# Feed-forwards: most column blocks as three 256-column matmuls per weight block, two blocks in one PSUM bank

## The reference, cut to what matters

```
D_MODEL = 1024
SEQ = 256
D_FF = 256 * ((8 * D_MODEL // 3 + 255) // 256)      # 2816

def rms_norm(x, g):
    xf = x.astype(jnp.float32)
    y = xf * lax.rsqrt(jnp.mean(xf * xf, axis=-1, keepdims=True) + EPS)
    return (y * g.astype(jnp.float32)).astype(x.dtype)

def swiglu(x, w_gate, w_up, w_down):
    return (jax.nn.silu(x @ w_gate) * (x @ w_up)) @ w_down

h = h + 0.5 * swiglu(rms_norm(h, ffn1_norm_g[layer]), ffn1_w_gate[layer],
                     ffn1_w_up[layer], ffn1_w_down[layer])
...
h = h + 0.5 * swiglu(rms_norm(h, ffn2_norm_g[layer]), ffn2_w_gate[layer],
                     ffn2_w_up[layer], ffn2_w_down[layer])
```

## Time and profile before

| | us |
|---|---|
| median of 3 runs | 1191.02 (1190.84 to 1191.08) |
| the profiled execution, whole | 1190.84 |
| its span, first to last instruction | 1189.2 |
| TensorE matmuls busy | 1179.6 (99%) |
| TensorE weight loads busy | 1044.4 (88%) |
| DVE busy | 862.4 (73%) |
| ACT busy | 677.6 (57%) |
| POOL busy | 65.6 (6%) |

### The profile page before, as it was taken

How to read it: one execution, slowest core, us unless ns; L and a number is a source line. 1 busy time by engine, 2 the same in 40 slices (tenths; PEclk the granted TensorE clock), 3 DMA queues, 4 the chain that set the end, 5 groups by cost and what they waited for, 6 DMA issues and landing times.

```text
span 1189.2 us, 18987 instructions
## 1 busy us (share of the span) xinstructions
PE 1179.6 (99%) x7592; PEld 1044.4 (88%) x7592; DVE 862.4 (73%) x1213; ACT 677.6 (57%) x1036; POOL 65.6 (6%) x86
## 2 busy tenths in 40 slices
PE   9999999999999999999999999999999999999998
PEld 8888889969888888888888888998888899779996
DVE  7877766887887767787766677677776668566875
ACT  6766654547655555655545457565554445556463
POOL 1501000200010000000000021000000000000000
PEclk9999999999999999999999999999999999999999
DMA  8865656663665556656655553256565665536450
GB/s 308 304 196 177 197 170 204 214 179 127 210 183 193 185 168 195 211 179 205 186 177 177 195 160 124 89 190 194 184 188 184 192 203 185 170 124 192 139 167 35
DMA packets 65398, 215.85 MB, mean 182 GB/s; under 512 B 8352, under 2 KB 12064, under 8 KB 65184
## 3 DMA queue, kind: packets, MB, share of 16 engines
q1 hardware_dynamic: 62608, 210.64, 55.3%
q10 hardware_dynamic: 2704, 4.02, 0.9%
HBM read 212.70 MB, written 1.93 MB: 180 GB/s over the span
## 4 chain that ended last, share of the span: by engine, by line
PE 95%; ACT 2%; DVE 1%; issue 1%; DMA 1%; SPq 0%; POOL 0%; ACTq 0%; POOLq 0%
PE psum L509 94%; DMA raw<-in_slots 1%; ACT whi L1249 1%; PE psum L918 0%; DVE wlo L1860 0%; ACT L1699 0%; ACT zob L1699 0%; DVE oa L2512 0%; PE psum L1058 0%; PE psum L878 0%; ACT qn L1568 0%; PE psum L1199 0%; PE psum L1007 0%; PE psum L968 0%; ACT pb L1568 0%
## 5 line engine op out<-in xcount | busy, mean ns | idle before, releaser
L509 PE MATMUL psum<-x,whi 128*128 128x512 f32 (+1 forms) x2512 | 633.7, 343 | 0.8 <-DVE aq L2447 0.3
L1860 DVE TENSOR_TENSOR wlo<-raw,whi 128x1024 fp32r<-128x1024 f32 (+2 forms) x402 | 474.1, 1191 | 167.6 <-ACT whi L1249 165.0
L1249 ACT CAST whi<-raw 128x1024 fp32r<-128x1024 f32 (+2 forms) x402 | 405.0, 1021 | 155.8 <-PE psum L509 150.8
L509 PE MATMUL psum<-x,wlo 128*128 128x256 f32 x1960 | 430.6, 279 | 0.0
L509 PEld LDWEIGHTS psum<-x,wlo 128*128 128x128 f32 x1960 | 366.6, 188 | 58.0 <-DVE wlo L1976 0.4
L509 PEld LDWEIGHTS psum<-x,whi 128*128 128x128 f32 x2512 | 382.2, 188 | 3.2 <-issue 1.3
L509 PE MATMUL psum<-g,whi 128*128 128x512 f32 x704 | 218.6, 392 | 0.0
L509 PEld LDWEIGHTS psum<-g,wlo 128*128 128x128 f32 x704 | 132.2, 188 | 29.5
L509 PE MATMUL psum<-whi,x 128*128 128x512 f32 (+1 forms) x512 | 140.6, 375 | 1.4 <-issue 1.4
L509 PE MATMUL psum<-g,wlo 128*128 128x256 f32 x704 | 139.0, 279 | 0.0
L509 PEld LDWEIGHTS psum<-g,whi 128*128 128x128 f32 x704 | 106.8, 188 | 0.0
(11 more groups left out here) (317 smaller groups left out, 775.8 us busy)
## 6 DMA issues: line engine op xcount, KB each, us to landing
raw<-in_slots SPq DMA_DIRECT2D x371, 512.0 KB, 4.1
raw<-in_slots SPq DMA_DIRECT2D x16, 384.0 KB, 3.4
raw<-in_slots SPq DMA_DIRECT2D x16, 256.0 KB, 2.9
h<-conv_mem SPq DMA_DIRECT2D x8, 284.0 KB, 5.5
mkv<-in_mem ACTq DMA_DIRECT2D x1, 1024.0 KB, 11.9
memt<-in_mem_cols ACTq DMA_DIRECT2D x1, 1024.0 KB, 15.1
conv_mem<-hc SPq DMA_DIRECT2D x3, 288.0 KB, 2.2
h<-conv_mem SPq DMA_DIRECT2D x4, 142.0 KB, 2.9
```

The costliest lines, as they stand in the source:

```text
L509: return pe.matmul(o, l, r, start=start, stop=stop, skip_group_check=True)
L1249: act.copy(held(B.whi[:, i % SPLIT, :], *n), held(B.raw[:, i % RAW, :], *n)).then_inc(*s.hi.now(i))
L1860: dve.tensor_tensor(held(B.wlo[:, i % SPLIT, :], *n), held(B.raw[:, i % RAW, :], *n), held(B.whi[:, i % SPLIT, :], *n).bitcast(F32), ALU.s ...
```

## The change

Two tables say which pairs of gate and up columns go in the narrow form: p = 2 to 6 in f = 0, p = 2, 3, 4 and 6 to 10 in f = 1, p = 2 to 10 in f = 2 and in f = 3. That is 5 + 8 + 9 + 9 = 31 pairs, 31 x 32 = 992 blocks. All 16 down pairs go narrow, 16 x 44 = 704 blocks. Together 1,696 of the feed-forwards' 2,112 blocks. p = 0 and p = 1 stay wide everywhere, p = 5 in f = 1, and p = 7 to 10 in f = 0.

A narrow gate pair lies whole in bank p % 2, an up pair in bank 2 + p % 2, so that two narrow pairs after each other use different banks. DVE reads them straight from PSUM: `gate_scale` and `up_mul` take the bank as an operand and wait for the slot's matmuls (`slot_used`), and down's first step does the same. For these 31 x 2 + 16 = 78 sums the ACT copy and the DVE sum are gone. TensorE waits (`read`) on the DVE step that read the bank two pairs before (or one, where forms change). The weights, their slots, splits and DMAs are as they were.

```
--- before.py
+++ after.py
@@ -39,6 +39,9 @@
 PAIRS = FF // 256
 
 LATE = 7
+
+NARROW_UP = (tuple(range(2, 7)), (2, 3, 4, 6, 7, 8, 9, 10), tuple(range(2, 11)), tuple(range(2, 11)))
+NARROW_DOWN = tuple(range(4))
 
 GAB_STEPS = (2, 2, 2, 1, 1, 2, 2, 1, 1, 1)
 
@@ -352,8 +355,8 @@
     sums = []
     for f in range(4):
         for p in range(PAIRS):
-            sums += [("gate", f, p), ("up", f, p)]
-        sums += [("down", f, p) for p in P4]
+            if p not in NARROW_UP[f]:
+                sums += [("gate", f, p), ("up", f, p)]
 
 
     s.w = [sig(f"w_in{i}", range(i, SLOTS, RAW), 16) for i in range(RAW)]
@@ -694,29 +697,47 @@
             mm(bank[7][:, i % 4 * 128:(i % 4 + 1) * 128], ones[:], ones[:], True, True)
 
 
-    def ffn(f, x, gen):
+    def read(done, part, f, p, narrow):
+
+        if p - 1 not in NARROW_UP[f]:
+            pe.wait_ge(*s.sum.at((part, f, p - 1)))
+        elif not narrow:
+            pe.wait_ge(*done.at((f, p - 1)))
+        elif p - 2 in NARROW_UP[f]:
+            pe.wait_ge(*done.at((f, p - 2)))
+
+    def ffn(f, xi, gen):
         base, F = FFN[f], B.ffn[f]
+        x = B.x[xi]
         for p in range(PAIRS):
             if f == 0 and p == LATE:
                 rows((rh[1], rl[1]), "mem0", 8, MKV0, 512, [[4], [5]])
+            narrow = p in NARROW_UP[f]
+            gate, up = (p % 2, 2 + p % 2) if narrow else (0, 2)
             if p:
-                pe.wait_ge(*s.sum.at(("gate", f, p - 1)))
+                read(s.gate, "gate", f, p, narrow)
             elif f == 1:
                 pe.wait_ge(*s.h.at((2, 0)))
             elif f == 2:
                 pe.wait_ge(*s.h.at((3, 2)))
             elif f == 3:
                 pe.wait_ge(*s.h.at((5, 0)))
-            if p:
-                cols(x, 8, up_slot(f, p), 0)
-                pe.wait_ge(*s.sum.at(("up", f, p - 1)))
-                cols(x, 8, up_slot(f, p) + 2, 2)
+            if narrow:
+                pair(xi, 0, up_slot(f, p), gate, range(4), True, False)
+                pair(xi, 0, up_slot(f, p) + 1, gate, range(4, 8), False, True)
+                read(s.mul, "up", f, p, narrow)
+                pair(xi, 0, up_slot(f, p) + 2, up, range(4), True, False)
+                pair(xi, 0, up_slot(f, p) + 3, up, range(4, 8), False, True)
+            elif p:
+                cols(x, 8, up_slot(f, p), gate)
+                read(s.mul, "up", f, p, narrow)
+                cols(x, 8, up_slot(f, p) + 2, up)
             else:
                 part(x, base, 0, range(4), True, False, gen)
                 if f in (1, 3):
                     pe.wait_ge(*s.h.at((2, 2) if f == 1 else (5, 1)))
                 elif f == 2:
-                    pe.wait_ge(*s.sum.at(("up", 1, PAIRS - 1)))
+                    pe.wait_ge(*s.mul.at((1, PAIRS - 1)))
                 part(x, base + 1, 2, range(4), True, False)
                 part(x, base + 2, 0, range(4, 8), False, True, gen)
                 part(x, base + 3, 2, range(4, 8), False, True)
@@ -726,7 +747,7 @@
             if f == 1 and p == 1:
                 pe.wait_ge(*s.kT0.at((1, 1)))
             if p == 2:
-                pe.wait_ge(*s.sum.at(("gate", f, PAIRS - 1)))
+                read(s.gate, "gate", f, PAIRS, False)
             if p == 3:
                 pe.wait_ge(*s.h.at(((1, 3, 4, 6)[f], 0)))
             down(f, F, down_slot(f, p), (4, 6, 0, 4)[p], p == 0)
@@ -743,7 +764,13 @@
                 if first and kc % 2 == 0:
                     pe.wait_ge(*s.g_hi.at((f, kc // 2)))
                     pe.wait_ge(*s.g_lo.at((f, kc // 2)))
-                t = two_blocks(b, h[:, k, :], l[:, k, :], F.g[:, kc], kc == 0, kc == 21, s.lo.at(i) if k == 0 else None)
+                for j in range(2):
+                    o, q = bank[b][:, j * S:(j + 1) * S], slice(j * 128, (j + 1) * 128)
+                    mm(o, h[:, k, q], F.gh[:, kc, :], kc + j == 0, False)
+                    mm(o, h[:, k, q], F.gl[:, kc, :], False, False)
+                    if k + j == 0:
+                        pe.wait_ge(*s.lo.at(i))
+                    t = mm(o, l[:, k, q], F.gh[:, kc, :], False, kc == 21)
             t.then_inc(*s.used.now(i))
             i += 1
 
@@ -1100,7 +1127,7 @@
 
     def second():
         X0 = (xh[0], xl[0])
-        pe.wait_ge(*s.sum.at(("up", 3, PAIRS - 1)))
+        pe.wait_ge(*s.mul.at((3, PAIRS - 1)))
         pair(0, 0, QK2, 2, range(4), True, False, "w2")
         pair(0, 0, QK2 + 1, 3, range(4), True, False)
         pair(0, 0, QK2 + 2, 2, range(4, 8), False, True, "w2")
@@ -1222,12 +1249,12 @@
                 t.then_inc(*s.tail.now((tt, j)))
 
     start()
-    ffn(0, B.x[0], "f0")
+    ffn(0, 0, "f0")
     mix_a()
-    ffn(1, B.x[1], "f1")
-    ffn(2, B.x[0], "f2")
+    ffn(1, 1, "f1")
+    ffn(2, 0, "f2")
     mix_b()
-    ffn(3, B.x[0], "f3")
+    ffn(3, 0, "f3")
     second()
 
 
@@ -1410,11 +1437,11 @@
                         gate_fn(0)
                         gate_fn(1)
                     up_rounded(0)
-                if i == 0 and p:
+                if i == 0 and p and p - 1 not in NARROW_UP[f]:
                     up_half(p - 1)
                 if i == 1 and p > 1:
                     up_rounded(p - 1)
-                if i == (2 if p else 1 if f == 0 else 3):
+                if i == (2 if p else 1 if f == 0 else 3) and p not in NARROW_UP[f]:
                     if p >= 2:
                         act.wait_ge(*s.mul.at((f, p - 2)))
                     half(("gate", f, p), up_slot(f, p) + (1 if p else 2), in_pairs(F.gr[:, p % 2, :]), 0)
@@ -1427,14 +1454,11 @@
                 use(up_slot(f, p) + i)
         for p in range(4):
             for i in range(6):
-                if p == 0 and i == 0:
+                if p == 0 and i == 0 and PAIRS - 1 not in NARROW_UP[f]:
                     up_half(PAIRS - 1)
                 if p == 0 and i == 1:
                     up_rounded(PAIRS - 1)
                 use(down_slot(f, p) + i)
-            if p >= 2:
-                act.wait_ge(*s.h.at((v, p - 2)))
-            half(("down", f, p), down_slot(f, p) + 5, in_pairs(B.htmp[:, p % 2, :]), (4, 6, 0, 4)[p])
             prep(v, p, targets)
 
 
@@ -1993,21 +2017,32 @@
         row = wide(row_of(n), 1, 2)
 
         def gate_sum(p):
+            if p in NARROW_UP[f]:
+                return
             halves(("gate", f, p), in_pairs(F.gr[:, p % 2, :]), 0)
 
         def gate_scale(p):
-            r = in_pairs(F.gr[:, p % 2, :])
+            r = q = in_pairs(F.gr[:, p % 2, :])
             if p == 0:
                 dve.wait_ge(*s.row.at(n))
-            dve.tensor_tensor(r, r, row, ALU.mult).then_inc(*s.gate.now((f, p)))
+            if p in NARROW_UP[f]:
+                dve.wait_ge(*s.used.at(up_slot(f, p) + 1))
+                q = in_pairs(bank[p % 2])
+            dve.tensor_tensor(r, q, row, ALU.mult).then_inc(*s.gate.now((f, p)))
 
         def up_sum(p):
+            if p in NARROW_UP[f]:
+                return
             halves(("up", f, p), in_pairs(F.pr[:, p % 2, :]), 2)
 
         def up_mul(p):
             r, q = F.gr[:, p % 2, :], F.pr[:, p % 2, :]
+            u = q
+            if p in NARROW_UP[f]:
+                dve.wait_ge(*s.used.at(up_slot(f, p) + 3))
+                u = bank[2 + p % 2]
             dve.wait_ge(*s.silu.at((f, p)))
-            dve.tensor_tensor(q, r, q, ALU.mult).then_inc(*s.mul.now((f, p)))
+            dve.tensor_tensor(q, r, u, ALU.mult).then_inc(*s.mul.now((f, p)))
 
         def up_rest(p):
             dve.wait_ge(*s.g_hi.at((f, p)))
@@ -2053,8 +2088,8 @@
                 use(down_slot(f, p) + i)
             tmp = in_pairs(B.htmp[:, p % 2, :])
             pair = flat(hT[:, 2 * p:2 * p + 2, :])
-            halves(("down", f, p), tmp, (4, 6, 0, 4)[p])
-            dve.scalar_tensor_tensor(out=tmp, in0=tmp, scalar=0.5, in1=row, op0=ALU.mult, op1=ALU.mult).then_inc(
+            dve.wait_ge(*s.used.at(down_slot(f, p) + 5))
+            dve.scalar_tensor_tensor(out=tmp, in0=in_pairs(bank[(4, 6, 0, 4)[p]]), scalar=0.5, in1=row, op0=ALU.mult, op1=ALU.mult).then_inc(
                 *s.dve_step.tick())
             dve.wait_ge(*s.dve_step.last())
             dve.tensor_tensor(pair, B.htmp[:, p % 2, :], pair, ALU.add).then_inc(*s.h.now((v, p)))
```

## The result

The kernel after took 1201.38 us (median; 1200.18 to 1205.49) beside 1191.05 us before (1190.84 to 1192.09), a ratio of 1.009 [1.0078, 1.0103]: 0.9% slower. The forecast was 1200.3 us. The profiled execution took 1200.59 us with a span of 1199.3.

The account below looks back on a forecast made before the run. TensorE, busy 99%, was taken to bound the kernel through distances between matmul starts. Block terms of -1.7, +7.1, +3.0 and +0.9 us gave +9.3 us on 1191.0: 1200.3 us, 8-in-10 range 1181.5 to 1203.0.

Parts of the forecast that it names:

- the sum's own terms: Narrow blocks: f = 0 -1.7 us; f = 1 to 3 gate and up +7.1, down +3.0 and +0.9; in all +9.3.
- the rival in which every narrow block is slow: All narrow blocks, f = 0 too, take the slow rhythm: +13.8 us, 1204.8 us; chance 0.07.
- Theory E: At entries, the wide form's two-kc cycle point sets the narrow rhythm; an odd number of extra kc turns it, even leaves it.
- Theory R: The rhythm belongs to the region (engines, DMAs or buffers there); extra kc or reordering turns no stretch.
- The copies and sums taken away are worth nothing: ACT loses 78 copies (45.8 us), DVE 78 sums (53.8 us); TensorE's work hides them, so the gain is nothing.
- New waits cost nothing: DVE's gate and up steps wait for TensorE's second slots, TensorE for banks two pairs back; cover suffices, cost zero.
- The price of a block: On x: wide 345.0 ns, narrow 340.0 or 353.5; narrow on g taken as on x.
- The rule of the entry: Where wide goes into narrow: last left pair spanning 0.39 us gives 340.0 ns blocks, 0.40 gives 353.5.
- that the trace of before tells how f = 0 will be entered: Last pairs of p = 1 and p = 10 in f = 0 span 0.39 us, so 336 blocks gain 1.7 us.
- quick everywhere: Rival: all narrow blocks quick, 1,520 gaining 5.0 ns and f = 2's 176 gaining 8.3: -9.1 us, 1181.9 us; chance 0.23.
- mixed: Rival: f = 1 from p = 6 and all f = 2 quick, rest as forecast: -1.6 us, 1189.4 us; chance 0.14.
- The estimate of 1195.2 us: N/2.4 + 2.5 ns per matmul: wide block 325 ns, narrow 327.5, change costs 4.2 us; the prediction set it aside.

Follow-up runs that it names:

- the other order: Kernel after with the last one or two wide kc ahead of four entries in f = 1 to 3 reordered, no work added: 1205.96 us.
- the first experiment: Kernel after with one or two extra wide kc ahead of five entries and one 256-column matmul ahead of f = 3 p = 2: 1198.98 us.

## Why f = 0 does not always come out the same

**Only f = 0 narrow.** The tables cut to f = 0, the rest in the wide form (the wide code put back for `down` of the other three).

```
-NARROW_UP = (tuple(range(2, 7)), (2, 3, 4, 6, 7, 8, 9, 10), tuple(range(2, 11)), tuple(range(2, 11)))
-NARROW_DOWN = tuple(range(4))
+NARROW_UP = (tuple(range(2, 7)), (), (), ())
+NARROW_DOWN = (0,)
```

> One part of the change alone: the narrow form in f=0 only (p=2 to 6 and down), all of f=1 to 3 wide as before. Forecast by the sum's own terms: 336 blocks x -5.0 ns = -1.7 us against before, 1189.4 us, and f=1 to 3 as long as before. If each added matmul had a cost wherever it stands (the rival in which every narrow block is slow) 336 x +8.5 ns = +2.9 us, 1194 us.

Ten executions, median 1193.95 us beside 1191.43; ratio 1.001 [0.9997, 1.0022]. They are no spread around one value but three clusters: 1188.8 (two), 1191.4 (two) and 1194.1 (six). The 1189.4 that the sum's own terms gave was met by the lowest cluster alone. The profiled execution was in the middle one, and had p = 2 to 6 slow and the down quick. 160 blocks of 13.3 ns are 2.1 us, the longer stall that starts them 0.1 (below), and 176 with the 24 that `mix_a` has behind them 2.7; by these sizes the clusters are none, one and both of f = 0's stretches slow. The two outer ones have no profile. The rival that every added matmul costs something had said 1194, which is near the median; but the quick down of the profiled execution contradicts it.

**The kernel after once more,** to see whether its own spread is this:

> The changed kernel, unchanged, for the spread of its times. If its f=0 falls either way in each execution (first stretch 160 blocks, second 176 and 24 of mix_a, 13.3 ns each), the times lie in clusters near 1200.3 (both quick), 1202.6 (one slow) and 1205.2 us (both slow). If something else scatters it, they lie in between as well.

1201.28 us (1200.72 to 1205.91), before beside it 1191.28; ratio 1.0092 [1.0073, 1.0111]. The profiled execution was the one of 1205.91. Its timeline around the break ahead of slot 7, where TensorE turns the norm row, and at the entry behind it:

```profile
26.54 0.39 PE L512 MATMUL psum<-x,wlo 128*128 128x256 f32 x2
26.92 0.43 PE L674 MATMUL psum<-ident,small 128*128 128x128 f32 x2
...
29.75 0.40 PE L512 MATMUL psum<-x,wlo 128*128 128x256 f32 x2
29.98 0.40 PE L512 MATMUL psum<-x,whi 128*128 128x256 f32 x2
...
85.81 0.40 PE L512 MATMUL psum<-x,whi 128*128 128x256 f32 x2
```

and the same break in the first profile of after:

```profile
27.41 0.40 PE L512 MATMUL psum<-x,wlo 128*128 128x256 f32 x2
27.65 0.38 PE L674 MATMUL psum<-ident,small 128*128 128x128 f32 x2
```

From the left pair to the row's matmul it is 0.38 us here and 0.24 there. These 0.14 us of waiting for the norm row turn the restart, the last left pair of p = 1 spans 0.40 in place of 0.39, and 160 blocks run at 55.83 us / 158 = 353.4 ns. The other profiles of kernels with x at these addresses agree: where the distance is 0.23 or 0.24 us (before, after, and the kernel with f = 0 wide below) p = 1 ends at 0.39; where it is 0.37 to 0.39 (this one, f = 0 alone, the other order, two nudges) it ends at 0.40, and in the first experiment, with 0.36 and one `kc` more, at 0.39. The down of f = 0 was slow too (at the break ahead of slot 45 the restart differed by some 3 ns), f = 1 to 3 were as in the first profile. So a stall that no table of waits lists costs 2 us, through the rhythm behind it. Both stretches slow are 5 us, and two of after's eight executions are 5 us above the lowest (1205.5, and the profiled 1205.9); five lie at 1200.2 to 1201.6. The one of 1202.16 has no profile, and I can't say which stretch it is. Why the highest cluster holds six of ten executions with f = 0 alone narrow, and two of eight here, is open.

## What the rhythm is worth once it is set by hand

**Two nudges.** The kernel after with one wide `kc` more ahead of p = 2 of f = 1 and of f = 3. f = 2 gets none; by the first run it should be handed the quick rhythm by f = 1.

```
+NUDGE = {105: 'dup1', 273: 'dup1'}
...
```

The code that reads the table is that of the first experiment.

> The changed kernel with one extra wide kc (4 matmuls into a free bank, never read, 0.7 us) ahead of f=1 p=2 and one ahead of f=3 p=2, nothing else. Theory E with what the first job showed (the quick rhythm is handed on from the narrow down of f=1 through the wide p=0 and p=1 of f=2): f=1, f=2 and f=3 all run at 0.340 us a block. Against before: 1,184 blocks x -5.0 ns and 176 x -8.3 ns in f=1 to 3 = -7.4 us, +1.4 us for the extra work, and f=0 as it falls: -1.7 us with both of its stretches quick, +0.6 with one slow, +2.9 with both slow. So times in three clusters at 1183.6, 1186 and 1188.3 us, median 1186 to 1188. Theory R: 1202 us or more.

1187.45 us (1185.51 to 1188.15) in five executions beside 1191.28; ratio 0.9963 [0.995, 0.9976]. Two `kc` of work that nobody needs made the kernel after 1.2% faster, and put it ahead of the kernel before. The timeline in f = 2, gate and up (282 blocks apart), then down (171 apart):

```profile
507.09 0.39 PE L513 MATMUL psum<-x,whi 128*128 128x256 f32 x2
...
602.97 0.39 PE L513 MATMUL psum<-x,whi 128*128 128x256 f32 x2
...
605.04 0.40 PE L513 MATMUL psum<-g,whi 128*128 128x256 f32 x2
...
665.92 0.40 PE L513 MATMUL psum<-g,whi 128*128 128x256 f32 x2
```

Gate and up are quick, 340.0 ns, handed on through the break between f = 1 and f = 2 as expected. But the down behind them, entered without a break out of the quick rhythm, runs at 60.88 us / 171 = 356.0 ns, the same as in after where it was entered slow. On this `g` the entry does not count.

**The same with f = 0 wide,** to be rid of its scatter (the tables start with `()` for f = 0, `NARROW_DOWN = (1, 2, 3)`):

> As n3_two_nudges, but f=0 wide as before the change, so that only f=1 to 3 are narrow. If f=0 alone makes the times fall into clusters, this one has a single cluster: -7.4 + 1.4 = -6.0 us against before, 1185.4 us within 0.5 us in each execution. If the small breaks in f=1 to 3 fall either way as well, it scatters by up to 6 us.

1187.96 us (1187.37 to 1188.97) in nine executions beside 1191.28; ratio 0.9973 [0.9963, 0.9983]. One cluster, as the reading of f = 0 wants it, though up to 1 us from its median and not the 0.5 that I had set. It missed the 1185.4 by 2.6 us, and the down of f = 2 explains that: 176 x (356.0 - 340.0) = 2.8 us. This term was still open.

## Why g of f = 2 is different: where it lies

What sets this `g` apart in the program is its address. Added up from the sizes of the tiles in the kernel (each begins at a multiple of 32 bytes), `x` and the `g` of f = 0, 1 and 3 lie 64 bytes past the weights (`whi`, `wlo`), modulo 256, and the `g` of f = 2 lies 128 past them. I call this the distance, +64 and +128. The weights stay where they are in all of the runs below, so they can't tell a distance from the weights from the place of the moving operand by itself; "distance" is only the name.

**Other distances.** The kernel after with `x` and `g` of f = 0 at distance 0, f = 1 at +128, f = 2 at +64, f = 3 at +192.

```
-        return [t[:, o:o + 8 * 2 * S].rearrange("p (k a n) -> p k a n", k=8, a=2) for o in (16, 0)]
+        return [t[:, o:o + 8 * 2 * S].rearrange("p (k a n) -> p k a n", k=8, a=2) for o in (0, 0)]
...
-        if f != 2:
-            sb(f"lead{f}", [128, 48], F32, c)
+        if (32, 0, 48, 80)[f]:
+            sb(f"lead{f}", [128, (32, 0, 48, 80)[f]], F32, c)
```

> The changed kernel with other addresses in SBUF for the moving operands, nothing else: modulo 256 bytes, relative to the weights, x moves from +64 to 0, g of f=0 from +64 to 0, g of f=1 from +64 to +128, g of f=2 from +128 to +64, g of f=3 from +64 to +192. Theory A (the rhythms come from weight reads and moving reads meeting, so that the distance of their addresses matters): blocks on x and on g change their time in either form, and down of f=2 loses the 2.7 to 3.3 ns a block by which it is slower than the other three. Theory B (addresses don't matter, the rhythm is one of the array's and the queue's alone): wide on x 345.0, narrow 340.0 or 353.3 ns a block everywhere, 1200 to 1205 us.

One execution: 1214.69 us beside 1191.28. The timeline, in this order: x at 0 (155 blocks apart), `g` of f = 1 at +128 (171), `g` of f = 2 at +64 (172), the first three pairs and a late one of `g` of f = 3 at +192 (174 from the second to the last):

```profile
380.22 0.40 PE L512 MATMUL psum<-x,whi 128*128 128x256 f32 x2
...
436.02 0.40 PE L512 MATMUL psum<-x,whi 128*128 128x256 f32 x2
...
437.09 0.40 PE L512 MATMUL psum<-g,whi 128*128 128x256 f32 x2
...
497.98 0.40 PE L512 MATMUL psum<-g,whi 128*128 128x256 f32 x2
...
626.03 0.40 PE L512 MATMUL psum<-g,whi 128*128 128x256 f32 x2
...
686.80 0.40 PE L512 MATMUL psum<-g,whi 128*128 128x256 f32 x2
...
926.36 0.40 PE L512 MATMUL psum<-g,whi 128*128 128x256 f32 x2
...
926.72 0.39 PE L512 MATMUL psum<-g,whi 128*128 128x256 f32 x2
...
985.88 0.39 PE L512 MATMUL psum<-g,whi 128*128 128x256 f32 x2
```

360.0 ns (55.80 us / 155), 356.1, 353.3, and 59.16 us / 174 = 340.0. The 356.0 moved with the distance from f = 2 to f = 1, so it belongs to +128 and not to the feed-forward. At 0 it is worst. At +192 something new happens: the stretch is entered out of the slow x, its first pair still spans 0.40, the second 0.39, and from there on it is quick. It healed itself. That is a distance at which the entry might not matter, so the next kernel has all operands there.

**The kernel after at +192, and the kernel before at +192.** The same four edits in both: the two views of each `x` tile exchange their offsets (`x` goes from 64 bytes to 0, the view that other code uses from 0 to 64), two small tiles go ahead of the first `x`, a pad and `first` go ahead of the second, and a longer tile goes ahead of `g` of f = 2. Tiles behind them, such as `ident`, move along. No instruction is added or moved.

```
-        return [t[:, o:o + 8 * 2 * S].rearrange("p (k a n) -> p k a n", k=8, a=2) for o in (16, 0)]
+        return [t[:, o:o + 8 * 2 * S].rearrange("p (k a n) -> p k a n", k=8, a=2) for o in (0, 16)]
...
+    B.ident4 = sb("ident4", [128, 32])
+    B.mhalf = sb("mhalf", [128, 16])
     x0, r0 = activations(0)
     B.maskb = sb("maskb", [128, 128], BF16)
-    B.ident4 = sb("ident4", [128, 32])
-    B.mhalf = sb("mhalf", [128, 16])
+    sb("pad", [128, 32])
+    B.first = sb("first", [128, 80 + 8 * S])
     x1, r1 = activations(1)
...
-    sb("even", [128, 4], F32, kv)
+    sb("even", [128, 52], F32, kv)
```

> The changed kernel with x and all four g at +192 bytes from the weights modulo 256 (they were at +64, g of f=2 at +128); a few small tensors change places for it, and nothing else. n5_addresses had only g of f=3 there, and its blocks went from 0.360 to 0.340 us by themselves. If that holds for x and g alike, all 1,696 narrow blocks run at 340.0 ns whatever the entry, and so do the narrow blocks outside the feed-forwards (some 470 that ran at 353): against the kernel before -9.1 us and -6.3 us, 1176 us with wide blocks still at 345.0, and a spread under 1 us, since no rhythm is left to choose. If it holds for g alone, x may be as bad as in n5_addresses (360 ns): 1200 us or more.

> The kernel before the change with the same addresses, and nothing else: what of n6_after_at_192 is owed to the addresses alone. Narrow blocks outside the feed-forwards go to 340 ns (-6.3 us) and down of f=2 to the 345 of the others (-0.6 us): 1184.4 us if wide blocks on x stay at 345.0; each ns of a wide block more or less moves it by 2.1 us. The difference to n6_after_at_192 is then the worth of the change itself at these addresses, 8 us by (345.0 - 340.0) ns x 1,696 blocks.

The changed kernel: **1179.89 us** (1179.76 to 1181.06) beside 1191.26; ratio 0.9909 [0.9894, 0.9924]. The kernel before: 1191.61 us (1191.18 to 1191.89); ratio 1.0004 [0.9995, 1.0013]. The first, at the entry of f = 1 (the last line 94 blocks on) and in the down of f = 2 (170 apart):

```profile
322.74 0.40 PE L513 MATMUL psum<-x,wlo 128*128 128x256 f32 x2
322.97 0.39 PE L513 MATMUL psum<-x,whi 128*128 128x256 f32 x2
...
354.93 0.39 PE L513 MATMUL psum<-x,whi 128*128 128x256 f32 x2
...
603.20 0.39 PE L513 MATMUL psum<-g,whi 128*128 128x256 f32 x2
...
661.00 0.39 PE L513 MATMUL psum<-g,whi 128*128 128x256 f32 x2
```

Both are 340.0 ns, and so are all 1,696 narrow blocks of the feed-forwards. The entry behind a left pair of 0.40 is quick here: the reading of the last pair holds at +64 only. The wide form has another cycle at this distance, in which every `kc` ends alike, its left pairs starting 118 or 119 ns apart. The kernel before at +192, wide on x in f = 2 (300 blocks apart) and on its `g` (170):

```profile
505.02 0.62 PE L510 MATMUL psum<-x,whi 128*128 128x512 f32 x2
...
609.02 0.62 PE L510 MATMUL psum<-x,whi 128*128 128x512 f32 x2
...
611.10 0.62 PE L510 MATMUL psum<-g,whi 128*128 128x512 f32 x2
...
670.04 0.62 PE L510 MATMUL psum<-g,whi 128*128 128x512 f32 x2
```

346.7 ns on both: 1.7 more than at +64, 1.8 less than at +128. Between the two kernels at the same addresses the change is worth 11.7 us, and 1,696 x (346.7 - 340.0) = 11.4 of it are in these rows. The addresses alone are, in sum, worth nothing to the kernel before, and 21.4 us to the kernel after (1201.3 to 1179.9, each beside a kernel before of 1191.3).

Both runs came out above what I had set. For the changed kernel that was 1176 us; its 416 wide blocks at 346.7 add 0.7, and 3.2 are left. For the kernel before it was 1184.4 and 2.1 us for each ns of a wide block, some 1188.0, and 3.6 are left. I had counted on every narrow stretch outside the feed-forwards turning quick, and not all did: the 48 blocks of `mix_a` that begin at 217.4 us in the one and at 220.1 in the other take 353.3 ns, where at +64 they took 340.0.

**Everything narrow at +192.** The same with p = 1 to 10 narrow in all four feed-forwards, 288 blocks more (and `mix_a` waits for the product of p = 10 in place of its sum):

```
+NARROW_UP = (tuple(range(1, 11)),) * 4
```

> As n6_after_at_192, with p=1 to 10 narrow in all four feed-forwards: 9 pairs more, 288 blocks at -5.0 ns, -1.4 us, 1174.5 us. If a narrow stretch that a small break interrupts fell back to the slow rhythm, it would be slower than n6_after_at_192 by up to 288 x 8.3 ns = 2.4 us and more in the pairs behind the breaks.

1181.82 us (1179.82 to 1183.24) beside 1191.26; ratio 0.9927 [0.991, 0.9943]: no gain over the kernel at +192 above, and more scatter. At 346.7 - 340.0 ns the 288 blocks should have given 1.9 us. The profile is of the quickest execution; in it most narrow stretches of the feed-forwards that begin behind a break heal within six matmuls, but two in f = 0 do not: 8 blocks in p = 1, and the 104 blocks behind the memory's rows, which stay at 353.3 ns to their end. So the quick rhythm at +192 is likely, not certain, when a narrow stretch begins behind a break; behind a wide `kc` it was quick at every entry.

## Why the prediction was right, point by point

- **TensorE bounds the kernel, and the distance between starts is the time.** Held: 99% busy, the same waits but for 0.4 us in the first 15, and the sum of block distances gives 9.4 of 10.1 us.
- **The copies and sums taken away are worth nothing.** Held. The page shows 48.1 and 43.7 us less of busy time, for the 53.8 and 45.8 that I counted from the means; either way it became idle time of DVE and ACT. The two kernels at +192 say how little even the extreme is: when TensorE gained 11.7 us, its listed waits did not grow (4.6 us in all, 5.2 in the kernel before at +192).
- **New waits cost nothing.** Held, no wait of PE on `gr` or `pr` in any trace.
- **The price of a block.** Held for x and for `g` of f = 1 and 3 (353.3, predicted 353.5) and for f = 0 (340.0). The price of the narrow form on `g`, for which I had no row and took that of x, was right in three of four. In f = 2 I allowed for "a few ns a block" on account of the wide form's 348.3 there; it was 2.5, or 0.4 us. What goes with it, the distance of +128, I did not see.
- **The rule of the entry.** Held in every one of the 40 places at +64 in which wide goes over into narrow without a break, in before, after and six of the runs: behind a last left pair of 0.39 us quick, behind 0.40 slow. Three of the 40 are no clean cases: two of the four reordered ends have no left pair, and in one place the single 256-column matmul stands between. Two places were few, but one added `kc` turned p = 2 of f = 1 in three runs of three and p = 2 of f = 3 in two of two, which a chance agreement would not do. What in the wide cycle is handed over the runs don't show; the span of the last pair is a mark of it. It differs by more than the starts: the quick pair's second matmul is listed at 276 ns and the slow one's at 280, where the prediction calls them the same.
- **What was wrong in it: that the trace of before tells how f = 0 will be entered.** "TensorE's program from each small break to the entry is unchanged" is true, and holds for f = 1 to 3, but the breaks in f = 0 restart either way from one execution to the next. The two quick stretches of the profile were luck: they give the sum its -1.7 us, and with f = 0 alone narrow the median of ten executions lies 2.5 us above before. The median of 1201.38 stands between executions with f = 0 quick and one that, by its time, has both stretches slow. I had given "all slow" 0.07, and two of eight executions of after were that, one by its profile (1205.9) and one by its time (1205.5). The kernel before hides this, since its wide blocks take 345.0 ns from whatever point they begin.
- **The rival "quick everywhere"** was a real state of this kernel, reached with two `kc` more, but its time was wrong: the 176 blocks of f = 2 lose 7.5 ns there in place of gaining 8.3. It would give 1191.05 - 7.6 + 1.3 = 1184.8 us, and the two quickest executions with the nudges (1185.5 and 1185.7, of which 1.4 are the nudges themselves) fit it with 1184.1 and 1184.3, if f = 0 was quick in them; neither has a profile.
- **The rival "mixed"** did not come: the break ahead of p = 5 of f = 1 restarted the wide cycle so that it ended slow behind slow blocks, and ended quick behind quick ones (in both kernels with nudges at f = 1 and f = 3 alone, which add nothing there). The rhythm is handed on through such a break, which the rival had as a coin toss.
- **A count in words.** The groups of 256-column matmuls grew by 3,392 records and those of 512 columns on x and `g` shrank by 1,696; the 1,696 that I announced are the difference.
- **The estimate of 1195.2 us** took its formula from the Trainium skill (TensorE: Matmul & The Clock Gate, "Back-to-back issue gap"). N/2.4 + 2.5 ns stands there for a single matmul; for a stream of loads and matmuls the section says that both set the spacing. So the miss says nothing against the formula as it is stated.

## What to carry to other kernels

Where TensorE bounds a kernel and nothing is waited for, read the distance between matmul starts stretch by stretch, since the same code can run in rhythms that are 4% apart. One execution shows only one of them: compare several. Before giving up a form of the loop as slower, try it with the moving operand 64, 128 and 192 bytes away from where it lies: here that turned +0.9% into -0.9%, at no instruction. And when executions of a kernel fall into clusters, look for a long stretch that starts behind a wait of varying length.

## What the runs showed of the hardware that I had not expected

- The time of a block of three 256-column fp32r matmuls depends on where the moving operand lies (as its distance from the weights, modulo 256 bytes): 360.0 ns at 0, 340.0 or 353.3 at +64 (by the entry), 356.0 at +128 behind a slow and behind a quick entry alike, 340.0 at +192 (in all stretches behind wide blocks; behind breaks 340.0 or 353.3). For the wide form it is 348.3 at 0, 345.0 at +64, 348.4 at +128 and 346.7 at +192. All at a granted clock of 0.999 and more. `x` and `g` at +64 lie 256 bytes apart modulo 512 and run alike, which is why I count modulo 256. The Trainium skill (SBUF — State Buffer, "A bandwidth-pool intuition that's wrong (but worth ruling out)") gives TensorE a second, independent read port for weight loads. It says nothing of addresses, so from it I would have expected no cost of where an operand lies; in these runs there is one (360.0 against 340.0 ns).
- A rhythm can be handed on over 280 us (with the nudges, from p = 2 of f = 1 to the down of f = 2), through wide stretches and breaks of some tenths of a us. Two `kc` that are thrown away bought 13.8 us, median against median.
- Why the place matters is open. The runs show that it does, at four distances for each form. Moving the weights in place of the moving operands, which would tell a distance from a place, was not tried.
